# Splitting weight slots in whole instructions instead of 512-column pieces on GpSimd, from the sparse layer's output product on

## The reference

```python
def even_layer(hn, ...):   ... hn @ w_in ... ; return concat([att, ssm]) @ w_out
def odd_layer(hn, ...):    ... hn @ w_in ... ; return (att * silu(gate)) @ w_out
for layer in range(2):
    xn = rmsnorm(h, norm_mix[layer]);  mn = rmsnorm(mem, norm_mem[layer])
    proj = xn @ w_in[layer];  km, vm = split(mn @ w_mem_kv[layer])
    log_f = log_sigmoid(f_logit + b_forget)          # first mixer; cumulated over positions
    h = h + merge_heads(concat([mix, mem_out])) @ w_out[layer]
    h = h + conv_ffn(rmsnorm(h, norm_ffn[layer]), w_up[layer], ..., w_down[layer])
return rmsnorm(h, norm_final)
```

## Time and profile before

| | us |
|---|---|
| median of 3 runs | 1864.41 (1863.04 to 1865.63) |
| the profiled execution, its own time | 1862.45 |
| its span, first to last instruction | 1860.6 |
| TensorE (PE) busy with matmuls | 1782.3, 96% of the span |
| VectorE (DVE) busy | 958.1, 51% |
| GpSimd (POOL) busy | 1014.6, 55%, in 1051 instructions |
| ScalarE (ACT) busy | 514.3, 28% |
| mean clock granted to TensorE | 0.986 of full speed |

### The profile page before, as it was taken

The page is one execution under the profiler, slowest core; times in us unless marked ns, Lnnn a source line. Parts: engine busy times, 40 slices in busy tenths (PEclk is TensorE's granted clock), DMA queues, the critical chain, the costliest instruction groups (busy, mean ns, idle before and its releaser), DMA issues.

```text
span 1860.6 us, 24417 instructions
## 1 busy us (share of the span) xinstructions
PE 1782.3 (96%) x9567; PEld 1408.9 (76%) x9572; DVE 958.1 (51%) x1928; ACT 514.3 (28%) x1144; POOL 1014.6 (55%) x1051
## 2 busy tenths in 40 slices
PE   7778999999899999999999999999999999999998
PEld 6565668767668886778888888887667798888886
DVE  5848575487453344542564156424666256514642
ACT  3430453321442234442211012122434322101111
POOL 7415145655317464335776767665343377667762
PEclk9989899999999999999999999999999999999999
DMA  6121312322124221211433333222112134233321
GB/s 183 35 69 46 114 46 70 101 69 80 40 71 132 82 91 46 69 46 46 131 91 103 91 97 107 79 91 91 46 46 65 50 97 119 85 90 109 91 92 56
DMA packets 173058, 151.68 MB, mean 82 GB/s; under 512 B 9304, under 2 KB 148056, under 8 KB 172944
## 3 DMA queue, kind: packets, MB, share of 16 engines
q1 hardware_dynamic: 172400, 149.69, 26.2%
q10 hardware_dynamic: 544, 0.44, 0.1%
HBM read 147.97 MB, written 2.14 MB: 81 GB/s over the span
## 4 chain that ended last, share of the span: by engine, by line
PE 86%; DVE 4%; POOL 1%; ACT 1%; issue 1%; another core or an unknown queue 0%; DVEq 0%; POOLq 0%; ACTq 0%
PE ps L279 72%; PE ps L1929 2%; PE ps L1962 2%; PE ps L1947 2%; PE ps L347 1%; POOL w_lo L131 1%; PE ps L1428 1%; PE ps L1406 1%; PE ps L1905 1%; PE ps L1935 1%; PE ps L1349 1%; PE ps L1357 1%; PE ps L652 0%; PE ps L1365 0%; PE ps L738 0%
## 5 line engine op out<-in xcount | busy, mean ns | idle before, releaser
L127 POOL TENSOR_SCALAR w_hi<-w_raw 128x512 fp32r<-128x512 f32 x522 | 314.0, 628 | 803.1 <-PE ps L279 740.1
L131 POOL TENSOR_TENSOR w_lo<-w_raw,w_hi 128x512 fp32r<-128x512 f32 x522 | 695.2, 1363 | 11.2
L279 PE MATMUL ps<-x_hi,w_hi 128*128 128x512 f32 (+1 forms) x1448 | 538.4, 372 | 0.9 <-POOL w_lo L131 0.7
L279 PE MATMUL ps<-x_lo,w_hi 128*128 128x512 f32 (+1 forms) x1448 | 527.8, 365 | 0.0
L279 PE MATMUL ps<-x_hi,w_lo 128*128 128x512 f32 (+1 forms) x1448 | 527.8, 364 | 0.0
L279 PEld LDWEIGHTS ps<-x_hi,w_hi 128*128 128x128 f32 x1448 | 274.8, 190 | 71.5 <-issue 21.5
L279 PEld LDWEIGHTS ps<-x_hi,w_lo 128*128 128x128 f32 x1448 | 274.6, 190 | 44.0
L279 PEld LDWEIGHTS ps<-x_lo,w_hi 128*128 128x128 f32 x1448 | 274.9, 190 | 40.8 <-issue 0.5
L2223 DVE SCALAR_TENSOR_TENSOR ffn_cv<-ps,col,ffn_cv 128x510 f32<-128x510 f32 (+1 forms) x176 | 131.8, 749 | 192.7 <-ACT ffn_cv L2201 188.1
L2201 ACT ACTIVATE ffn_cv<-ps,col 128x512 f32<-128x512 f32 x88 | 63.7, 775 | 500.2 <-PE ps L279 500.2
L307 DVE TENSOR_TENSOR h<-h,ps 128x512 f32<-128x512 f32 x64 | 43.9, 688 | 271.0 <-PE ps L279 270.9
(11 more groups left out here) (326 smaller groups left out, 2454.6 us busy)
## 6 DMA issues: line engine op xcount, KB each, us to landing
w_raw<-w_up SPq DMA_DIRECT2D x88, 512.0 KB, 5.1
w_raw<-w_down SPq DMA_DIRECT2D x16, 1024.0 KB, 5.0
w_raw<-od_w_in SPq DMA_DIRECT2D x12, 1024.0 KB, 5.3
w_raw<-w_in_fox SPq DMA_DIRECT2D x10, 1024.0 KB, 5.3
w_raw<-w_in_dil SPq DMA_DIRECT2D x10, 1024.0 KB, 5.0
w_raw<-ev_w_in SPq DMA_DIRECT2D x8, 1024.0 KB, 7.7
w_raw<-w_out SPq DMA_DIRECT2D x8, 1024.0 KB, 5.0
w_raw<-w_down SPq DMA_DIRECT2D x8, 768.0 KB, 4.4
```

Source lines behind the costliest of these rows:

```text
L127: ins = pool.tensor_scalar(hi[:, c:min(c + PIECE, size)], raw[:, c:min(c + PIECE, size)], 1.0, 1.0, ALU.mult, ALU.mult)
L131: ins = pool.tensor_tensor(lo[:, c:min(c + PIECE, size)], raw[:, c:min(c + PIECE, size)], hi[:, c:min(c + PIECE, size)].bitcast(F32), ALU. ...
L279: mm = pe.matmul(o, l, r, start=start and i == 0, stop=stop and i == 2)
```

## The change

`split` does pieces of 512 columns only for slots below `whole_from`, which is set to the first slot of the sparse layer's output product, 29. From there on each slot is split by one TENSOR_SCALAR and one TENSOR_TENSOR over all its columns: 2048 in 96 of the 105 slots, 1024 in the forget gate's and 1536 in the last of each half of the down product.

```diff
@@ class Weights @@
+        self.whole_from = 0
@@ def split @@
-            for c in range(0, size, PIECE):
-                ins = pool.tensor_scalar(hi[:, c:min(c + PIECE, size)], raw[:, c:min(c + PIECE, size)], 1.0, 1.0, ALU.mult, ALU.mult)
+            piece = PIECE if n < self.whole_from else size
+            for c in range(0, size, piece):
+                ins = pool.tensor_scalar(hi[:, c:min(c + piece, size)], raw[:, c:min(c + piece, size)], 1.0, 1.0, ALU.mult, ALU.mult)
             ins.then_inc(self.hi_done, 1)
             pool.wait_ge(self.hi_done, n + 1)
-            for c in range(0, size, PIECE):
-                ins = pool.tensor_tensor(lo[:, c:min(c + PIECE, size)], raw[:, c:min(c + PIECE, size)], hi[:, c:min(c + PIECE, size)].bitcast(F32), ALU.subtract)
+            for c in range(0, size, piece):
+                ins = pool.tensor_tensor(lo[:, c:min(c + piece, size)], raw[:, c:min(c + piece, size)], hi[:, c:min(c + piece, size)].bitcast(F32), ALU.subtract)
             ins.then_inc(self.split_done, 1)
@@ block_kernel @@
         w_od_out = [deep_half(t["od_w_out"][0], 0, 0, KD), 0]
+        W.whole_from = w_od_out[0]
```

## The result

The changed kernel takes 1870.74 us (median of 6 runs, 1869.98 to 1871.18), the kernel before, on the same chip, 1864.04 (6 runs, 1862.18 to 1865.63). The ratio is 1.0036, with a 95% interval of 1.0025 to 1.0046: slower by 6.7 us, 4.7 to 8.6. The profiled execution has a span of 1868.9 us, against 1860.6.

A forecast was written before the change was run, and what follows sets the result against it. TensorE, busy for 96% of the span, was taken as the bound, so GpSimd edits count only through its waits. Terms -3.0 + 2.9 + 1.7 + 0.5 + 1.0 + 4.2 = +7.3 us gave median 1871.7, range 1860 to 1879.

The forecast's parts named there:

- the likeliest case: Whole kernel: the forecast itself, median 1871.7 us with a range of its own from 1868 to 1875; chance 0.42.
- the hold for the length of one GpSimd instruction: VectorE's SBUF-to-SBUF rows wait until GpSimd's instruction under way ends; longest hold 4.59 us instead of 1.29.
- slot 31: Sparse layer: VectorE's row of 384 columns ends 1.6 us later, TensorE's second wait ends 0.5 later: +0.5 (0 to 1.6).
- the clock: TensorE at half clock after waits: +1.7 us behind slot 29 (ends 0 and 2.1), -0.4 behind slot 36.
- slot 29: Sparse layer's output product: VectorE waits for the whole subtraction, TensorE's wait grows from 2.4 to 5.3 us: +2.9.
- The rival that GpSimd lets VectorE in: Long GpSimd instructions leave room for VectorE, so no wait grows: -5.1 us, 1859.3, faster; chance 0.17.
- the forget gate: Slots 40 to 43: VectorE's rows are held, its last subtraction waits for a copy, `cum` comes later: +1.0 us.
- the second mixer: Last rope tile, slot 91: VectorE's sum waits for GpSimd's whole subtraction, logits and TensorE come later: +4.2 us.
- slot 36: Memory, slots 34 to 36 back to back: shorter slots cut TensorE's wait from 5.7 to 3.1 us: -2.6.
- Nothing in the steady steps and in the networks: Mixers' steady steps and feed-forward networks: VectorE's idleness covers the holds: 0, up to 1 us in all for the mixers.
- The race: Forget gate: VectorE's cast comes about 0.3 us before slot 43's copy; the rival, losing it, gives 1878.0; chance 0.23.
- The third rival: Slots 29 and 91: long hold falls beside VectorE's work and the clock stays up: +1.4 us, 1865.8; chance 0.18.

The follow-up runs named there:

- the second trace of before: The kernel before with one added line that sets a number nobody reads, no instruction differing, run and profiled again; two such kernels measured 1864.28 and 1864.61 us.
- experiment 3: The changed kernel, but with slots 40 and 41 in pieces, so that slot 42 ends about 1.8 us later: 1877.41 us, +13.2 against the kernel before.

## Why the prediction was right, and where it was not

1871.7 was forecast and 1870.74 measured, +7.3 against +6.7, in the likeliest case. The mechanism, the hold for the length of one GpSimd instruction, is borne out. Of the terms, four of five waits were right to 0.3 us; slot 31 and the clock were not. The waits were forecast at +6.0 in sum and came to +4.6, the clock at +1.3 and came to +2.2 or +2.6, by which trace of before it is held against. That the two errors nearly cancel is luck.

- **Lengths.** 1.90 and 4.59 us expected, 1.92 and 4.61 measured. That the cost is linear in the columns beyond 512 is shown (1.05 and 2.38 at 1024 columns, 1.48 and 3.51 at 1536).
- **The hold.** A VectorE row of 4.1 us at slot 29 was named as the sign; it took 4.05, and that of slot 91, expected at about 5, took 4.87. The rival that GpSimd lets VectorE in would have shown a row ending before 477 in the first trace's time: it ended at 480.20, 478.95 in that time. By the rule of the Trainium skill, SBUF — State Buffer, section "SBUF: two separate sides", the hold lasts the whole instruction, and the trace agrees, now for a subtraction of 4.50 us, which that row outlasts by 0.08.
- **The waits.** TensorE's waits grew by 2.8 at slot 29 (predicted 2.9), 0.7 at the forget gate (1.0) and 4.0 before the second mixer (4.2), and shrank by 2.6 for slot 36 (2.6). At slot 31 I had put +0.5; one wait of 2.47 took the place of 0.91 and 1.90, so it is -0.3. VectorE's row of 384 columns did end 1.6 later, as I had it, and the first wait, which I had left out, grew by that much. The step that failed is that the second wait stays and ends 0.5 later: it is gone, since VectorE's next rows (`finish`) come behind GpSimd's subtraction and are no longer held by pieces (the last of them takes 0.69 instead of 1.65).
- **Nothing in the steady steps and in the networks** is right to 0.1 us up to slot 133, and the kernel with 84 such slots shows +0.2 (-1.5 to +1.9). The cover is real: in the first network VectorE's three rows behind each tile took 1000, 1223 and 1486 ns before, and 2277, 427 and 692 after, so one long wait in place of three short ones.
- **The clock** was wrong as a step. I had +1.7 behind slot 29 and -0.4 behind slot 36 and neutral elsewhere, +1.3 in sum. Against the second trace of before, the five windows give +0.4, 0, -2.5, +1.7 and +2.6, in sum +2.2; against the first trace the sum is +2.6. I had read the full clock behind slot 29's 2.43 us as a property of the short wait, and two more traces of the same kernel have it halved there. Likewise the half clock before the second mixer, which I took for given, is absent in both. With one trace the clock behind a short wait can't be costed to better than some 1.7 us each way, and the range that I gave for slot 29, 0 to 2.1, belongs to each wait of up to 3.1 us, in the kernel before as in the changed one. Behind the changed kernel's 5.20 and 6.69 us a half clock was right to expect (see below).
- **The race** at the forget gate was won by 0.06 us (the cast's issue against the copy's start), where I had 0.3. The four traces with slots 40 to 42 whole won it, by 0.06, 0.34, 0.05 and 0.04, so it was close but not a single draw. Lost, it gives 1877.4 (experiment 3), where the rival had 1878.0. A chance of 0.23 for it was fair, or low: what decided is less than a cast's length.
- **The third rival**, that the hold falls beside VectorE's work, needed the order at slot 91 to be the other way round. With the copy in pieces it is, and the wait stays at 2.69.

Open is what sets the clock behind a given wait. Its length alone doesn't: behind 1.70 us at slot 29 it stayed full, behind 1.97 it was halved, behind 2.43 it did both; behind 3.1 us for slot 36 it was full twice and halved five times (the kernel with every slot whole counted). Only for long waits is there no exception: in the fourteen traces TensorE waits 21 times for 3.2 us or more from slot 28 on, and the 8 us behind each have a granted clock of 0.80 or less. Half clock elsewhere, and what TensorE did ahead of the wait, weren't varied by themselves.

## What to carry to other kernels

Merging instructions on GpSimd saves its own time, 0.8 us of 7.4 for a slot here, and lengthens the longest time that VectorE's SBUF-to-SBUF work can be held, from 1.3 to 4.6 us. So merge only where TensorE waits for GpSimd, and keep pieces short where TensorE waits for VectorE: seven whole slots of 105 (32 to 38) brought the gain, and four (29, 42, 43 and 91) the longer waits. And take a second trace of the same kernel before a granted clock behind a single short wait is counted as cause or effect.

## What the runs showed of the hardware

- VectorE's rows that read one operand from PSUM are not held: the product from PSUM at 1287.79 took 0.69 us beside a GpSimd copy, and the 132 rows of the networks' convolution (L2226) that lie for nine tenths or more within GpSimd's instructions in the changed kernel took 747 to 751 ns each. Nor are a reciprocal of one column (0.16 us at 475.95, within slot 29's subtraction), a fill in the kernel with the lost race (0.48 us at 674.35, within slot 42's) and the search's MAX8 in the kernel with every slot whole (0.43 us at 411.66, within slot 24's).
- Being short doesn't help a row that is held: with every slot whole, a TENSOR_TENSOR of one column from SBUF to SBUF took 4.17 us at 219.29, within slot 11's subtraction.
- VectorE gets in between two instructions of GpSimd that follow each other, with one row at a time: at the lost race the row issued at 679.78 ends 0.27 us behind the copy's end, though the subtraction follows, and the cast issued at 681.76 ends 0.27 behind the subtraction's. So this chain of dependent rows paid once for each instruction of GpSimd that it met, and in the networks, where GpSimd has one long instruction in the way, one of three rows paid (2277, 427 and 692 ns).
- At slots 34 to 36 the starts of copy and subtraction, 592.54, 594.55, 599.13, 601.13 and 605.70, follow each other by the lengths that the profile gives plus 0.08 or less 0.03 us, so that spans on GpSimd can be added up here.
- The same instructions with the same waits at the five places had half clock behind slot 36, the forget gate and the second mixer in the first trace of the kernel before, and behind slots 29, 31 and 36 in the other two, which were taken on one chip and agree with each other; the first one's chip is not on record. From slot 28 to the end the three take 1407.8, 1408.3 and 1408.4 us all the same: what was lost at one place was saved at another. In the kernel that is whole from slot 32 and in the one with pieces at 91, the scatter of the times goes with the mean granted clock, which fits half-clock stretches that come and go and don't cancel; the faster runs have no trace that would show it.
